# Another order of turns, scores and scale factors in the attention stage of a one-core Macaron block

## The chip, the cores and the metric

The kernel runs on one core of a Trainium2 chip. The metric is the device time of one execution in microseconds (us). Three runs of the kernel before are shown, and their median is compared.

## What is computed

One transformer block on 512 tokens of width 1024: a layer norm, half a SwiGLU feed-forward, a token mixer, and the other half feed-forward, each closed by a layer norm and modulated by nine vectors from a small product of the conditioning vector. All of it is fp32. The change is in the token mixer:

```python
z = h @ w_mix_in                   # pool, q, k/v of three branches, gates
y_a = pool_mixer(u_pool, pool_w, pool_scale) @ w_branch_a
y_b = nsa_attention(q, k_cmp, v_cmp, k_slc, v_slc, k_win, v_win, g_nsa, ...) @ w_branch_b
return (g_a * y_a + g_b * y_b) @ w_mix_out
# nsa_attention: 8 heads of 64, 2 key/value groups
#   o = g0 * softmax(q kc^T + bias) vc  +  g1 * softmax(q kslc^T + bias) vslc
#     + g2 * softmax(q kwin^T + bias) vwin
```

With 512 tokens, blocks of 64, 16 blocks selected and a window of 512, the selected and the window branch are both plain causal attention over all 512 keys. The compressed branch has 31 keys.

## The kernel before

**Weights.** Each product in fp32 is made of three: high part by high part, high by low, low by high. A panel of 128x1024 weights is loaded by the queue of SyncE into one of two `raw` buffers, ScalarE makes its high part (L1147), GpSimd its low part (L539), TensorE multiplies it with the 512 tokens (L616 to L618, 24 matmuls). Panels are taken in the order of the list `MIX`, then the branch panels (`B_BRANCH`, ...), and counted by `panels_used`. GpSimd works through its own list in order: splits, `alibi(j)` (the position bias of a pair of heads, L564), and `normalize(u)` (L574).

**Before the loop.** After panel `q3`, TensorE makes the compressed keys and values (L932, L936). VectorE copies them to `kcB` and `VC` (L1976, L1979) and counts `cmp_kv_taken`. Then follow panel `kslc`, the compressed scores of all heads (L947, waits for `cmp_kv_taken`), panel `kwin`, the scores of unit 0, panel `vslc`, the pool mixer's product, panel `vwin`, the transposes of the compressed probabilities (L998) and those of the two values (L1006, each waits until ScalarE has copied its panel out of PSUM, L1453).

**The loop.** It goes over eight units: four pairs of heads by two branches (`PAIR_UNITS`). A unit has four tiles of 128 queries, tile t with 128(t+1) keys, for two heads. For each unit and tile:

- `score(u, t)`, TensorE, L976: two products into PSUM banks 0 and 1 or 2 and 3, by turns.
- `shift(u, t)`, VectorE, L2012: adds the bias, keeps the row's extreme, writes to `Pr` in SBUF.
- `exps(u, t)`, ScalarE, L1431: the exponential, with the row's sum.
- `scales(u, part)`, VectorE, L2021 and L2023: one over the sum, times the gate, for the tiles of that part. `scales(u, 2)` also multiplies tile 3 by its factors (L2031).
- `normalize(u)`, GpSimd, L574: multiplies tiles 0, 1, 2 of both heads, six instructions.
- `turn(u, i)`, TensorE, L1027: transposes, in six turns given by `TURNS`; turn i goes to bank 4, 5 or 7 (`TURN_BANK[i % 3]`), so that turn i waits until turn i - 3 has been copied out.
- `take_turned(u, i)`, ScalarE (L1442) or VectorE (L2041): copies the turned tile to `PT`.
- `weigh(u)`, TensorE, L1054, for the first branch of a pair with L1041 ahead: the product with the values into bank 6. After a pair, `take_heads` (L1446 on ScalarE, L2045 on VectorE) empties the bank.

Step s of the loop handles unit s in its scores, unit s-1 in its turns and unit s-2 in `weigh`. The order of every engine is written out by hand. Before the change it is, in step s:

```text
TensorE  score(s,0) weigh(s-2) score(s,1) score(s,2) turn(s-1,0..3) score(s,3) turn(s-1,4) turn(s-1,5)
VectorE  shift(s,0) scales(s-1,2) shift(s,1) take(2) shift(s,2) scales(s,0) take(3) [heads] shift(s,3) scales(s,1)
ScalarE  exps(s,0) [heads] take(0) take(1) exps(s,1) exps(s,2) take(4) take(5) [split] exps(s,3)
GpSimd   normalize(s-1), then an alibi or a split in some steps
```

In step 8, which has no scores, panel `B_BRANCH` stands where the scores would. After the loop come the branch panels and `weigh(7)`.

Of the kernel before, what the change touches and what calls it, by code (L numbers as in the profile page):

```python
# [35 lines left out]
P = 128  # L36
# [25 lines left out]
       "vslc", "poolw", "vwin"]  # L62
# [25 lines left out]
TURNS = [(0, (0, 1)), (1, (0, 1)), (3, (0,)), (3, (1,)), (2, (0,)), (2, (1,))]  # L88
# [88 lines left out]
def build(nc, xT, cols, ada_w, ada1, ffn_in, ffn_out, mix_w, pool_w, branch_w, mixout_w,  # L177
          w1, w2, pos, ident_in, dist_in, cbias_in, cmask_in, icnt_in, out):
    with ExitStack() as ctx:
# [349 lines left out]
        def _(gp):  # L529
# [37 lines left out]
            def normalize(u):  # L567

                for t in range(TT - 1):
                    gp.wait_ge(scales_made, 3 * u + 1 + t // 2)  # L570
# [41 lines left out]
        def _(pe):  # L612
# [328 lines left out]
            k8_panel("kslc")  # L941
            pe.wait_ge(cmp_kv_taken, 2)
            pe.wait_ge(act_evac, MIX8.index("q3") - 1)
            for t in range(TT):
# [4 lines left out]
                if t % 2:  # L949
                    ins.then_inc(cmp_scored, 1)  # L950
            k8_panel("kwin")
# [31 lines left out]
            pe.wait_ge(shifted, 6)  # L983
# [9 lines left out]
            k8_panel("vwin")  # L993
# [8 lines left out]
            pe.wait_ge(shifted, 8)  # L1002
            for v in range(2):
                pe.wait_ge(act_evac, MIX8.index("vslc") - 1 + v)
                for t in range(TT):
                    ins = pe.transpose(psum[:, 2 + v, P * t:P * t + P], vT[:, v, t * P:(t + 1) * P], ident[:, :])  # L1006
                ins.then_inc(v_turned, 1)

            def turn(u, i):
# [22 lines left out]
            def weigh(u):  # L1032
# [10 lines left out]
                pe.wait_ge(turned_act, 4 * u + 4)  # L1043
                pe.wait_ge(turned_dve, 2 * u + 2)
# [14 lines left out]
            for s in range(1, NPU + 1):  # L1059
# [14 lines left out]
                turn(s - 1, 4)  # L1074
                turn(s - 1, 5)

            for m in range(KT):
                p = B_BRANCH + 3 * m
                b = 4 * (m % 2)
                if m >= 2:  # L1080
                    pe.wait_ge(br_mixed, m - 1)
                if m == 1:
                    pe.wait_ge(o_split, HPG)
                if m:
                    panel_over_h(p, p % 4, b)
# [48 lines left out]
        def _(act):  # L1134
# [281 lines left out]

            def take_k(br, name):
# [3 lines left out]
            take_k(0, "kslc")  # L1421
            act.wait_ge(cmp_shifted, 1)
            act.activation(Pc[:, :, :, 0:N_CMP], Pc[:, :, :, 0:N_CMP], ACT.Exp).then_inc(cmp_exp, 1)
# [794 lines left out]
```

## Time and profile before

| | |
|---|---|
| median of 3 runs | 1132.77 us (1132.46 to 1132.92) |
| the profiled execution | 1132.92 us, span 1131.1 us |
| TensorE busy | 1106.7 us, 98% of the span |
| GpSimd, VectorE, ScalarE busy | 529.4, 512.6, 409.3 us |
| attention loop, 500.47 to 569.52 us | 69.05 us, TensorE busy 62.98 us |

The span is from the first to the last instruction. Busy time is the union of an engine's instructions. A wait is idle time of an engine just ahead of an instruction, with what ended it. In a timeline each row is one instruction or a run of equal ones: start, length, engine, line, operation, output and inputs, count, and in brackets the idle time ahead and its releaser. The first shape of a run stands for all of it.

### The profile page before, as it was taken

How to read it: one execution, taken by the hardware profiler on the slowest of the kernel's cores; microseconds unless marked ns; L12 is line 12 of the kernel's file. 1: busy time of each engine (PE TensorE's matmuls, PEld its weight loads, DVE VectorE, ACT ScalarE, POOL GpSimd, SP SyncE). 2: the span in 40 equal slices, each digit the busy share in tenths (PEclk: the TensorE clock that was granted, in tenths of full speed). 3: DMA queues.
4: the chain of work that ended last, by engine and by line, in shares of the span. 5: the costliest groups of instructions: out<-in, count | busy, mean ns of one | idle time of the engine just before them, and what ended most of it. 6: DMA issues, size and time to landing. Idle time of an engine off the chain costs nothing.

```text
span 1131.1 us, 15426 instructions
## 1 busy us (share of the span) xinstructions
PE 1106.7 (98%) x5596; PEld 905.2 (80%) x5596; DVE 512.6 (45%) x888; ACT 409.3 (36%) x649; POOL 529.4 (47%) x274
## 2 busy tenths in 40 slices
PE   7999999999999999999999999999999999999997
PEld 4788888888888897865578888888888888888886
DVE  5577755311221368368837775774322221211113
ACT  4452332233222283267723232347232222322222
POOL 1435544444445464459814543546544544444440
PEclk9999999999999999999999999999999999999999
DMA  9455554323333262210036654323443333233322
GB/s 374 153 190 209 185 191 168 102 94 96 88 90 99 79 249 92 84 36 21 22 128 214 202 174 155 112 75 112 134 136 121 111 111 96 90 98 91 99 68 75
DMA packets 52372, 142.13 MB, mean 126 GB/s; under 512 B 5728, under 2 KB 11872, under 8 KB 51040
## 3 DMA queue, kind: packets, MB, share of 16 engines
q1 hardware_dynamic: 51312, 136.25, 36.6%
q10 hardware_dynamic: 1008, 5.17, 1.2%
q8 instruction: 34, 0.56, 0.2%
q14 instruction: 18, 0.15, 0.0%
HBM read 139.31 MB, written 2.10 MB: 125 GB/s over the span
## 4 chain that ended last, share of the span: by engine, by line
PE 93%; DVE 4%; issue 1%; ACT 1%; DMA 0%; ACTq 0%; DVEq 0%
PE psum L616 29%; PE psum L618 28%; PE psum L617 28%; PE psum L1054 2%; PE psum L1027 1%; PE psum L976 1%; PE psum L911 1%; PE psum L633 1%; PE psum L647 0%; DMA X<-in_xT 0%; DVE Pr L2012 0%; DVE X L1664 0%; PE psum L668 0%; DVE scr L1604 0%; PE psum L723 0%
## 5 line engine op out<-in xcount | busy, mean ns | idle before, releaser
L539 POOL TENSOR_TENSOR w_lo<-raw,w_hi 128x1024 fp32r<-128x1024 f32 x184 | 452.8, 2465 | 535.1 <-ACT w_hi L1147 534.7
L616 PE MATMUL psum<-h_hi,w_hi 128*128 128x512 f32 (+1 forms) x1016 | 384.9, 379 | 1.3 <-DVE h_lo L1677 0.8
L618 PE MATMUL psum<-h_hi,w_lo 128*128 128x512 f32 (+1 forms) x1016 | 381.9, 376 | 0.0
L617 PE MATMUL psum<-h_lo,w_hi 128*128 128x512 f32 (+1 forms) x1016 | 381.7, 376 | 0.0
L1147 ACT ACTIVATE w_hi<-raw 128x1024 fp32r<-128x1024 f32 x184 | 192.9, 1051 | 150.6 <-PE psum L618 99.0
L616 PEld LDWEIGHTS psum<-h_hi,w_hi 128*128 128x128 f32 x1016 | 191.1, 188 | 40.1 <-issue 3.0
L618 PEld LDWEIGHTS psum<-h_hi,w_lo 128*128 128x128 f32 x1016 | 191.1, 188 | 35.1
L617 PEld LDWEIGHTS psum<-h_lo,w_hi 128*128 128x128 f32 x1016 | 191.2, 188 | 33.9
L1760 DVE SCALAR_TENSOR_TENSOR acc<-ada_raw,cact,acc 128x512 f32<-128x512 f32 x98 | 137.7, 1440 | 18.1 <-DMA ada_raw<-in_ada_w 17.9
L616 PE MATMUL psum<-act_hi,w_hi 128*128 128x512 f32 (+1 forms) x374 | 141.4, 378 | 0.9 <-issue 0.9
L618 PE MATMUL psum<-act_hi,w_lo 128*128 128x512 f32 (+1 forms) x374 | 140.9, 377 | 0.0
L617 PE MATMUL psum<-act_lo,w_hi 128*128 128x512 f32 (+1 forms) x374 | 140.8, 377 | 0.0
L1830 DVE SCALAR_TENSOR_TENSOR X<-psum,mod,X 128x512 f32<-128x512 f32 x20 | 15.0, 750 | 194.9 <-PE psum L618 194.9
L1317 ACT ACTIVATE act_hi<-scr 128x512 f32 (+1 forms) x42 | 26.6, 632 | 190.6 <-DVE scr L1791 190.6
L616 PEld LDWEIGHTS psum<-act_hi,w_hi 128*128 128x128 f32 x374 | 70.4, 188 | 14.0 <-issue 1.3
L1781 DVE SCALAR_TENSOR_TENSOR scr<-scr,psum 128x512 f32<-128x512 f32 x44 | 30.1, 685 | 113.0 <-ACT scr L1324 113.0
L618 PEld LDWEIGHTS psum<-act_hi,w_lo 128*128 128x128 f32 x374 | 70.4, 188 | 13.0
L617 PEld LDWEIGHTS psum<-act_lo,w_hi 128*128 128x128 f32 x374 | 70.4, 188 | 12.7
L1791 DVE TENSOR_TENSOR scr<-scr,psum 128x512 f32<-128x512 f32 x44 | 30.2, 686 | 92.9 <-PE psum L618 92.7
L1324 ACT ACTIVATE scr<-psum 128x512 f32<-128x512 f32 x44 | 26.1, 594 | 88.3 <-PE psum L618 88.3
L1772 DVE TENSOR_TENSOR act_lo<-scr,act_hi 128x512 f32 (+1 forms) x44 | 33.2, 754 | 36.3 <-ACT act_hi L1317 34.9
L574 POOL TENSOR_SCALAR Pr<-Pr,pscl 128x128 f32<-128x128 f32 (+2 forms) x48 | 44.9, 955 | 8.9 <-DVE pscl L2023 8.8
(240 smaller groups left out, 1000.8 us busy)
## 6 DMA issues: line engine op xcount, KB each, us to landing
raw<-in_ffn_in SPq DMA_DIRECT2D x82, 512.0 KB, 3.3
ada_raw<-in_ada_w SPq DMA_DIRECT2D x112, 256.0 KB, 3.5
raw<-in_ffn_out SPq DMA_DIRECT2D x32, 448.0 KB, 3.4
raw<-in_mix_w SPq DMA_DIRECT2D x27, 512.0 KB, 3.3
ada_first<-in_ada SPq DMA_DIRECT2D x8, 1024.0 KB, 11.5
raw<-in_ffn_out SPq DMA_DIRECT2D x16, 512.0 KB, 3.5
raw<-in_branch_w SPq DMA_DIRECT2D x8, 512.0 KB, 4.0
raw<-in_mixout_w SPq DMA_DIRECT2D x8, 512.0 KB, 3.3
```

What stands on the lines that cost most here:

```text
L539: gp.tensor_tensor(w_lo[:, slot, :], raw[:, slot % 2, :], w_hi[:, slot, :].bitcast(F32), ALU.subtract).then_inc(split_done, 1)
L574: gp.tensor_scalar(pr, pr, pscl[:, n:n + 1], None, ALU.mult).then_inc(probs_pool, 1)
L616: pe.matmul(o_, w_hi[:, wslot, ws], xh, start=first, stop=False)
L617: pe.matmul(o_, w_hi[:, wslot, ws], xl, start=False, stop=False)
L618: return pe.matmul(o_, w_lo[:, wslot, ws], xh, start=False, stop=last)
L1147: act.activation(w_hi[:, slot, :], raw[:, slot % 2, :], ACT.Copy).then_inc(split_hi, 1)
L1317: act.activation(act_hi[:, c - 1, :] if isinstance(c, int) else act_hi[:, bass.ds(c - 1, 1), :].rearrange("p o t -> p (o t)"), scr[:, 1 - ...
L1324: act.activation(scr[:, c2, :], bank(2 * c2 if b is None else b), ACT.Tanh, scale=0.5).then_inc(tanh_done, 1)
L1760: dve.scalar_tensor_tensor(a, ada_raw[:, q % 3, :], sc, a, ALU.mult, ALU.add).then_inc(ada_used, 1)
L1772: dve.tensor_tensor(lo_, scr[:, b, :], hi.bitcast(F32), ALU.subtract).then_inc(act_split, 1)
L1781: dve.scalar_tensor_tensor(scr[:, c2, :], scr[:, c2, :], 1.0, bank(b0), ALU.add, ALU.mult).then_inc(gated, 1)
L1791: dve.tensor_tensor(scr[:, c2, :], scr[:, c2, :], bank(b0 + 1), ALU.mult).then_inc(hidden_made, 1)
```

## The change

- `MIX`: `vwin` is taken before `poolw`, and TensorE runs `vslc`, `vwin`, the transposes of the values, and only then the pool product and the transposes of the compressed probabilities. VectorE's copies follow that order.
- TensorE makes the compressed scores straight after the compressed keys and values; panel `kslc` follows them.
- VectorE finishes the compressed probabilities before the shifts of unit 0 instead of after them.
- `TURNS` takes tile 2 (turns 2 and 3) before tile 3 (turns 4 and 5). VectorE copies out turns 0, 1 and 5, ScalarE 2, 3 and 4.
- `scales` has two parts instead of three: tiles 0 to 2, then tile 3. The first is issued after `take_turned(s-1, 5)`, ahead of `shift(s, 3)`. `normalize` waits once, for the first part.
- Step 8 of the loop has no panel; `B_BRANCH` comes after the loop, ahead of `B_BRANCH + 1` and `weigh(7)`.

In step s of the loop the orders become:

```text
TensorE  score(s,0) weigh(s-2) score(s,1) turn(s-1,0) turn(s-1,1) score(s,2) turn(s-1,2..5) score(s,3)
VectorE  shift(s,0) scales(s-1,1) shift(s,1) take(0) take(1) shift(s,2) take(5) [heads] scales(s,0) shift(s,3)
ScalarE  exps(s,0) [heads] exps(s,1) take(2) take(3) take(4) exps(s,2) [split] exps(s,3)
```

The core of the diff:

```diff
-       "vslc", "poolw", "vwin"]
+       "vslc", "vwin", "poolw"]
...
-TURNS = [(0, (0, 1)), (1, (0, 1)), (3, (0,)), (3, (1,)), (2, (0,)), (2, (1,))]
+TURNS = [(0, (0, 1)), (1, (0, 1)), (2, (0,)), (2, (1,)), (3, (0,)), (3, (1,))]
...
+                gp.wait_ge(scales_made, 2 * u + 1)
                 for t in range(TT - 1):
-                    gp.wait_ge(scales_made, 3 * u + 1 + t // 2)
...
-            k8_panel("kslc")
             pe.wait_ge(cmp_kv_taken, 2)
...
+            k8_panel("kslc")
             k8_panel("kwin")
...
             k8_panel("vslc")
-            pe.wait_ge(shifted, 6)
+            k8_panel("vwin")
+            pe.wait_ge(shifted, 8)
+            for v in range(2):
+                pe.wait_ge(act_evac, MIX8.index("vslc") - 1 + v)
+                for t in range(TT):
+                    ins = pe.transpose(psum[:, 2 + v, P * t:P * t + P], vT[:, v, t * P:(t + 1) * P], ident[:, :])
+                ins.then_inc(v_turned, 1)
...
-                elif i in (0, 5):
-                    pe.wait_ge(turned_dve, 2 * u + i // 5)
+                elif i in (0, 1, 5):
+                    pe.wait_ge(turned_act, 3 * u + (-1, 0, 0, 0, 0, 1)[i])
                 else:
-                    pe.wait_ge(turned_act, 4 * u + (0, -1, 0, 1, 2)[i])
+                    pe.wait_ge(turned_dve, 3 * u + i - 2)
...
                 if s < NPU:
                     score(s, 1)
+                turn(s - 1, 0)
+                turn(s - 1, 1)
+                if s < NPU:
                     score(s, 2)
-                else:
-                    pe.wait_ge(shifted, 8 * NPU)
-                    panel_over_h(B_BRANCH, B_BRANCH % 4, 0)
-                for i in range(4):
+                for i in range(2, 6):
                     turn(s - 1, i)
                 if s < NPU:
                     score(s, 3)
-                turn(s - 1, 4)
-                turn(s - 1, 5)
...
-                ts = (slice(0, 2), slice(2, 3), slice(3, 4))[part]
+                ts = slice(0, 3) if part == 0 else slice(3, 4)
...
+            for v in range(2):
+                dve.wait_ge(v_turned, v + 1)
+                dve.tensor_copy(V[:, v, :, :].rearrange("p t c -> p (t c)"), bank(2 + v)).then_inc(v_taken, 1)
             for g in range(4):
                 dve.wait_ge(poolout_hi, g + 1)
...
                 if s <= NPU:
-                    take_turned(s - 1, 2)
+                    take_turned(s - 1, 0)
+                    take_turned(s - 1, 1)
                 if s < NPU:
                     shift(s, 2)
-                    scales(s, 0)
                 if s <= NPU:
-                    take_turned(s - 1, 3)
+                    take_turned(s - 1, 5)
                 if s >= 3 and s % 2:
                     take_heads((s - 3) // 2)
                 if s < NPU:
+                    scales(s, 0)
                     shift(s, 3)
-                    scales(s, 1)
```

## Rows read from the trace of the kernel before

**Rows 1.** The page of the profile: the span, and the busy time of each engine.

```profile
span 1131.1 us, 15426 instructions
...
PE 1106.7 (98%) x5596; PEld 905.2 (80%) x5596; DVE 512.6 (45%) x888; ACT 409.3 (36%) x649; POOL 529.4 (47%) x274
```

**Rows 2.** The waits of TensorE over the span: total us, times, longest us.

```profile
PE psum L1041 <- DVE o_lo L2045: 2.1, 3, 1.0
PE psum L1054 <- ACT PT L1442: 2.0, 3, 0.7
...
PE psum L1054 <- DVE PT L2041: 1.0, 1, 1.0
PE psum L976 <- DVE V L2072: 0.9, 1, 0.9
```

**Rows 3.** Busy time by stretch: the attention loop, then steps 4 and 5 of it.

```profile
500.47:569.52 69.05, 62.98 (x405) 37.08 (x405) 53.69 (x188) 47.49 (x145) 57.42 (x52) 1.00 0.11 36
524.58:533.77 9.19, 8.62 (x57) 4.69 (x56) 7.67 (x28) 6.30 (x21) 8.57 (x9) 1.00 0.00 0
533.77:542.08 8.31, 7.62 (x53) 4.50 (x52) 6.68 (x27) 7.63 (x23) 7.96 (x8) 1.00 0.00 0
```

**Rows 4.** Timeline, TensorE: compression products, the kslc panel's start, compressed scores.

```profile
467.23 0.63 PE L936 MATMUL psum<-w2s,hidden 128*31 128x64 f32 x8
467.80 0.50 PE L616 MATMUL psum<-h_hi,w_hi 128*128 128x512 f32 x1
...
473.37 3.68 PE L947 MATMUL psum<-kcB,qT 128*128 128x62 f32 x32
```

**Rows 5.** Timeline, VectorE: the four copies into VC.

```profile
468.33 1.17 DVE L1979 TENSOR_SCALAR VC<-psum 31x128 f32<-31x128 f32 x4
```

**Rows 6.** Timeline, TensorE and ScalarE: what follows the vwin panel; its copy from PSUM.

```profile
498.63 1.03 PE L998 MATMUL psum<-ident,Pc 128*128 128x128 f32 x8
...
498.83 0.60 ACT L1453 ACTIVATE vT<-psum 128x512 f32<-128x512 f32 x1 [3.81 <-PE psum L618]
```

**Rows 7.** Timeline, TensorE, in step 5 of the loop.

```profile
534.96 2.38 PE L1054 MATMUL psum<-PT,V 128*64 128x512 f32 x16 [0.69 <-ACT PT L1442]
...
538.54 1.75 PE L1027 MATMUL psum<-ident,Pr 128*128 128x128 f32 x14
540.22 1.13 PE L976 MATMUL psum<-kT,qT 64*128 64x512 f32 x4
```

**Rows 8.** Timeline, the other engines in the same steps.

```profile
532.85 0.62 ACT L1431 ACTIVATE Pr<-Pr,nmax 128x384 f32<-128x384 f32 x1
...
533.41 0.17 DVE L2023 TENSOR_TENSOR pscl<-pscl,G 128x4 f32<-128x4 f32 x1
...
533.68 5.61 POOL L574 TENSOR_SCALAR Pr<-Pr,pscl 128x128 f32<-128x128 f32 x6 [0.45 <-DVE pscl L2023]
...
533.97 0.19 ACT L1431 ACTIVATION_READ_ACCUMULATOR Pr<-Pr,nmax 128x1 f32 x1
...
539.08 1.03 ACT L1442 ACTIVATE PT<-psum 128x256 f32<-128x256 f32 x2 [0.56 <-PE psum L1027]
```

**Rows 9.** Groups by shape, 505 to 562 us: count, then busy us and mean ns.

```profile
L1431 ACT ACTIVATE Pr<-Pr,nmax 128x512 f32<-128x512 f32 x14 | 10.0, 714 | 3.5 <-DVE nmax L2012 3.5
...
L2012 DVE CUSTOM_DVE_ANT_0 Pr<-psum,abias 128x512 f32<-128x512 f32 x14 | 9.0, 681 | 0.0
...
L1431 ACT ACTIVATE Pr<-Pr,nmax 128x256 f32<-128x256 f32 x14 | 6.9, 498 | 0.0
...
L1442 ACT ACTIVATE PT<-psum 128x512 f32<-128x512 f32 x6 | 3.6, 598 | 0.3
```

**Rows 10.** Duration in ns, min/median/max: the scales' product; VectorE's normalising of tile 3.

```profile
L2023 DVE TENSOR_TENSOR pscl<-pscl,G x24: 160/163/2180, 486.7 to 563.0; 128x2 f32<-128x2 f32 x16, 128x4 f32<-128x4 f32 x8
...
L2031 DVE TENSOR_SCALAR Pr<-Pr,pscl x16: 485/794/811, 488.6 to 563.9; 128x512 f32<-128x512 f32 x16
```

More of the change, by code:

```diff
@@ L991, in _ @@
             ins.then_inc(panels_used, 1)
-            k8_panel("vwin")
             pe.wait_ge(cmp_probs, 1)
@@ L1001, in _ @@
                 ins.then_inc(cmp_PT, 1)
[L1002 to L1007, printed above, removed]
             def turn(u, i):
@@ L1081, in _ @@
                     pe.wait_ge(br_mixed, m - 1)
+                if m == 0:
+                    pe.wait_ge(shifted, 8 * NPU)
                 if m == 1:
                     pe.wait_ge(o_split, HPG)
-                if m:
-                    panel_over_h(p, p % 4, b)
+                panel_over_h(p, p % 4, b)
                 panel_over_h(p + 1, (p + 1) % 4, b + 1)
@@ L1415, in _ @@
             take_q(3)
-            def take_k(br, name):
+            act.wait_ge(cmp_shifted, 1)
+            act.activation(Pc[:, :, :, 0:N_CMP], Pc[:, :, :, 0:N_CMP], ACT.Exp).then_inc(cmp_exp, 1)
+            for br, name in enumerate(("kslc", "kwin")):
                 wait_used(taken(name))
                 act.activation(kT[:, br, :], bank(MIX_BANK[name]), ACT.Copy).then_inc(act_evac, 1)
-            take_k(0, "kslc")
-            act.wait_ge(cmp_shifted, 1)
-            act.activation(Pc[:, :, :, 0:N_CMP], Pc[:, :, :, 0:N_CMP], ACT.Exp).then_inc(cmp_exp, 1)
-            take_k(1, "kwin")
             def exps(u, t):
@@ L1449, in _ @@
                 exps(0, t)
-            def take_v(v, name):
-                act.wait_ge(panels_used, taken(name))
+            for v, name in enumerate(("vslc", "vwin")):
+                wait_used(taken(name))
                 act.activation(vT[:, v, :], bank(MIX_BANK[name]), ACT.Copy).then_inc(act_evac, 1)
-            split_before(taken("vslc"))
-            take_v(0, "vslc")
             for g in range(4):
@@ L1460, in _ @@
                                scale=colv[:, C_PSCALE + g:C_PSCALE + g + 1]).then_inc(poolout_hi, 1)
-            split_before(B_BRANCH - 1)
-            take_v(1, "vwin")
             for s in range(1, NPU + 1):
@@ L1468, in _ @@
                     take_heads((s - 3) // 2)
-                take_turned(s - 1, 0)
-                take_turned(s - 1, 1)
                 if s < NPU:
                     exps(s, 1)
+                for i in range(2, 5):
+                    take_turned(s - 1, i)
+                if s < NPU:
                     exps(s, 2)
-                take_turned(s - 1, 4)
-                take_turned(s - 1, 5)
                 if s in (4, 6):
@@ L2001, in _ @@
             dve.tensor_tensor(Pm, Pm, over_blocks(cst[:, 0, :]), ALU.subtract).then_inc(cmp_shifted, 1)
+            dve.wait_ge(gates_taken, 1)
+            seen = cmask[:, :, 0:1].broadcast_to([P, TT, HEADS])
+            link(dve.tensor_tensor(cst[:, 2, :].rearrange("p (t h) -> p t h", t=TT), G[:, :, 0:24:3], seen, ALU.mult))
+            dve.wait_ge(cmp_exp, 1)
+            link(dve.tensor_reduce(cst[:, 1, :], Pv, AX.X, ALU.add))
+            link(dve.reciprocal(cst[:, 1, :], cst[:, 1, :]))
+            link(dve.tensor_tensor(cst[:, 2, :], cst[:, 1, :], cst[:, 2, :], ALU.mult))
+            dve.tensor_tensor(Pm, Pm, over_blocks(cst[:, 2, :]), ALU.mult).then_inc(cmp_probs, 1)
             def shift(u, t):
@@ L2025, in scales @@
                                   G[:, ts, c:c + 3 * HPG + 1:3 * HPG], ALU.mult).then_inc(scales_made, 1)
-                if part == 2:
-                    dve.wait_ge(scales_made, 3 * u + 3)
+                if part == 1:
+                    dve.wait_ge(scales_made, 2 * u + 2)
                     for hd in range(2):
@@ L2069, in _ @@
                 dve.tensor_copy(PcT[:, g, :], bank(4 + g)).then_inc(cmp_PT_taken, 1)
-            for v in range(2):
-                dve.wait_ge(v_turned, v + 1)
-                dve.tensor_copy(V[:, v, :, :].rearrange("p t c -> p (t c)"), bank(2 + v)).then_inc(v_taken, 1)
             for s in range(1, NPU + 2):
@@ L2077, in _ @@
                 if 2 <= s <= NPU:
-                    scales(s - 1, 2)
+                    scales(s - 1, 1)
                 if s < NPU:
```

13 lines of the change are left out of this document (2 added, 11 removed).

## The prediction

> **What bounds the kernel now.** I read the page first: TensorE is busy for 1106.7 of 1131.1 us [rows 1], and it is the chain that ends last. So the change can give or take only what TensorE waits. Its waits by line come next: those that touch the change are 2.1 us at L1041, 2.0 and 1.0 at L1054, 0.9 at L976 [rows 2], 6.0 together. The windows put them in the attention loop: 69.05 us long, 62.98 busy, so 6.07 us idle; the granted clock there is 1.00, the level of 2.4 GHz [rows 3]. Step 4, with the compressed product, holds 8.62 us of work in 9.19, step 5 holds 7.62 in 8.31 [rows 3]: the mean step has 8.12 us of work and 0.63 of waiting. Nothing else that is edited touches a wait of TensorE today. The timelines of one step then give the prices [rows 4 to 8].
>
> **The parts ahead of the loop.** *Compressed scores before `kslc`.* L936 ends at 467.86 and `kslc` starts at 467.80 (starts overlap ends a little) [rows 4]. The scores wait for `cmp_kv_taken`, and the last of VectorE's copies to `VC` ends at 468.33 + 1.17 = 469.50 [rows 5]. Today the panel, 473.37 - 467.80 = 5.57 us, hides this. Moved ahead of it, the scores start at about 469.55: **+1.75 us**. Behind the waiting TensorE stand `kslc`, `kwin` and the scores of unit 0; all move by as much. What is late next: nothing, since ScalarE's exponential and VectorE's sums get the `kslc` and `kwin` panels as cover, 11 us. For the same reason the compressed probabilities, moved ahead of unit 0's shifts on VectorE, cost nothing; without that cover they would hold back the shifts by some 3 us.
>
> *`vwin` and the value transposes ahead of the pool product.* ScalarE starts to copy `vwin` 0.20 us after the panel's end (498.63, where the next product starts) and needs 0.60 [rows 6]. Today the compressed transposes cover it. Now only the four transposes of `vslc` stand between, 0.48 at 0.12 each (14 of them take 540.22 - 538.54 = 1.68 us [rows 7]). **+0.35 us**: 0.85 - 0.48.
>
> *The first step of the loop.* Today TensorE waits 0.9 us in it for VectorE's copies of V [rows 2]. Now those are done early, but the pool product stands right ahead, and VectorE's four subtractions and two copies behind it have to end before `shift(1, 0)`, on which `score(1, 2)` waits for its bank. I found about 0.8 to 1.0 us; I let it cost 0.9, as today. Bounds: 0 and 2.
>
> **The loop.** The gain that the change has is plain. Today `weigh` waits 0.69 us for ScalarE's last copy [rows 7] or for `take_heads`. With `score(s, 3)` behind the last turn there is about 1.1 us more of cover [rows 7], and these waits, 0.6 to 1.0 in each of steps 2 to 8, go.
>
> But a new cycle appears. `scales(s, 0)` now needs the exponentials of tile 2; on ScalarE these stand behind the copy of turn 4; turn 4 stands on TensorE behind turn 3, and turn 3 needs the last of GpSimd's six multiplications of unit s-1, which start only with `scales(s-1, 0)`. Today none of these steps closes the circle: GpSimd starts on tiles 0 and 1 before tile 2 is known, and turn 2 is a tile that VectorE normalises. One turn round this ring:
>
> - from the end of `scales` to GpSimd's start: 533.68 - 533.58 = 0.10 [rows 8]
> - six multiplications: 5.61 [rows 8]
> - from GpSimd to TensorE: not seen as a wait in the trace. Between 0 and 0.2, the size of the other handovers here; I take 0.1
> - turn 3 (three transposes) and turn 4 (four): 0.84
> - to ScalarE's copy: the first turn's two transposes begin at 538.54, end at 538.78, and the copy starts at 539.08 [rows 7, 8]: 0.30
> - copy of 512 columns: 0.60 [rows 9]
> - two exponentials of 384: 532.85 to 534.16: 1.31 [rows 8]
> - reciprocal and product of `scales`, twice 0.17 and the gap between [rows 8]: 0.40
>
> Sum 9.26; I use **9.25 us** a step, 9.0 to 9.5 with the bounds. TensorE has 8.12, so GpSimd's chain is the new bound. Other edits of the loop lie within it: VectorE has the copies of turns 0, 1, 5 instead of 2 and 3, the same engine's work of about 7 us a step [rows 3]; `scales(s-1, 1)` and the normalising of tile 3 end some 4 us after the ring's start, and their turn comes at 6.2. An alibi or a split of GpSimd, up to 3 us, fits in the 3.6 us for which it waits in the ring.
>
> From the end of `score(1, 3)` to that of `score(7, 3)` there are six rounds, 55.5 us. TensorE's work in them is 3 x 8.62 + 3 x 7.62 = 48.7 [rows 3]: 6.8 us of waiting. Step 8: `score(7, 3)` ends 1.05 us before `scales(7, 0)` does; then 0.1 + 5.61 + 0.1 to turn 3, and turns 3, 4, 5 take 1.32: 8.2 us, with `weigh(6)` 2.3, the compressed product 1.0 [rows 3] and 2.4 of transposes as work: 2.4 us of waiting. Panel `B_BRANCH`, which stood in this step, is only moved. It sat ahead of the turns and hid this wait; without it nothing does. After the loop `weigh(7)` comes after the same sum of work as today, so what hangs on it (VectorE's units of the modulation, SyncE's loads) keeps its place.
>
> **The sum.** Waits in the loop: 0.9 + 6.8 + 2.4 = 10.1, less 6.07 now: +4.0. With 1.75 and 0.35: +6.1. I take off 0.1 for roundings: **+6.0 us**. The profiled execution has 1132.92 us, 1.8 more than its span, and gives 1138.9; the median is 0.15 below it: **1138.8 us**.
>
> **A rule weighed.** VectorE's product in `scales` has a median of 0.163 us, and once took 2.18 [rows 10], while GpSimd subtracted 1024 columns. With GpSimd's multiplications under way it is mostly the short value; the normalising of tile 3 beside them varies from 0.485 to 0.811. The Trainium skill (SBUF — State Buffer, "Who interferes with whom") has a VectorE instruction with two SBUF inputs, or in a two-port mode, shut out for the whole of a GpSimd instruction that reads SBUF. The trace agrees for the one long case and not for most of the others.
>
> **Rivals.**
> - *The ring does not close as I say, and the next one binds.* It runs between VectorE and ScalarE: `shift(s-1, 3)` to its first half, 0.7, two exponentials of 512, 1.5 [rows 9], `scales` 0.4, normalising 1.4 [rows 10], half of `shift(s, 1)` 0.45, two exponentials of 256 1.0, three copies 1.45, two exponentials of 384 1.31, `scales` 0.4: 8.6 us. For it speaks that GpSimd's times are rough; against it, that 5.6 us for six tiles returns in every step. 6.0 - 6 x 0.6 = +2.4: 1135.2 us.
> - *Faster.* The last turn's copy leaves the path, and no ring is longer than TensorE's 8.12 us. Left are 2.1 us ahead of the loop, 0.9 in step 1 and 1.0 at the end, less 6.07: -2.0 us, 1130.8. It decides for faster once a round takes less than 8.25 us, 1.0 below my sum; GpSimd alone has 5.6 of it, and the copy and the exponentials 1.9. I see no term that could lose so much.
> - *GpSimd shuts VectorE out.* `scales(s-1, 1)` and the normalising fall under GpSimd's multiplications. If they waited for whole instructions, by the 2 us of the one long case, VectorE's copy of turn 1 would come 1.5 us after turn 4's place, and each round grow by that: +9 more, 1148 us. Against it: both already lie under GpSimd's work today, at a median of 0.163 and 0.794 [rows 10].
>
> **How the numbers follow.** Chances: forecast 0.71, the next ring 0.16, faster or even 0.08, shut out 0.05. The forecast's own range, by the ring's bounds (six rounds by 0.25) and the first step's, is 1136.9 to 1140.6. Eight times in ten: from 1134.8, with the next ring in it, to 1141.0. About 0.2%, 2.3 us, is what a measurement of this kernel can tell from no change. Slower by more: the forecast, the shut-out and a third of the next ring, 0.81. Within: the rest of that ring and part of the even case, 0.14. Faster: 0.05.
>
> **What would show it.** Right: L947 starts about 1.7 us after L936 ends; in steps 2 to 7 the times between two `score(s, 3)` are near 9.25 for odd and even steps alike; TensorE waits at L1027 for GpSimd's L574, and no longer at L1054 for L1442; GpSimd starts 0.1 us after `scales` in each step. The loop with its waits has 10 us idle. Wrong: steps of 8.3 and 8.6 us (a ring of another kind), waits at L976 for VectorE's shift, or a wait at L947 that is not there because the copies to `VC` are quicker.

## The result

The changed kernel takes 1141.61 us (median of 4 runs, 1141.44 to 1141.84) where the kernel before takes 1132.85 beside it (1132.46 to 1134.3): a ratio of 1.0076, with an interval of 1.0057 to 1.0093. It is slower, as forecast, by 8.8 us where 6.0 were forecast. 1138.8 was named, with a range to 1141.0, and the time lies 0.6 above it. The question of the experiments is where the 2.8 us more come from; the answer begins with the fact that the forecast's 6.0 was not right in its parts either.

The profiled execution took 1139.34 us, 2.3 less than the median; what the record says of that difference stands under "Open" below. The page of the profile of after, to be held against [rows 1]:

```profile
span 1137.3 us, 15410 instructions
PE 1111.6 (98%) x5596; PEld 907.3 (80%) x5596; DVE 515.3 (45%) x880; ACT 407.0 (36%) x641; POOL 530.0 (47%) x274
```

TensorE has the same 5,596 matmuls and is **busy for 4.9 us more**: 1111.6 against 1106.7. A change that only moves work can't do that if a matmul always takes the same time. Its idle time rose by only 1.3 us (1137.3 - 1111.6 = 25.7, before 24.4). The waits of TensorE from 440 to 600 us, to be held against [rows 2] (total us, times, longest us):

```profile
PE psum L1027 <- POOL Pr L574: 2.6, 5, 0.7
PE psum L1027 <- DVE PT L2037: 1.9, 3, 0.6
PE psum L946 <- DVE VC L1966: 1.7, 1, 1.7
PE psum L1041 <- DVE o_lo L2041: 0.7, 3, 0.4
PE psum L1027 <- DVE PcT L2057: 0.7, 2, 0.5
PE psum L988 <- ACT vT L1446: 0.3, 1, 0.3
```

The waits at L1054 are gone. New are those of the turns (L1027), the 1.7 at the compressed scores (L946, the line that was L947) and the 0.3 at the value transposes (L988): 7.9 us in all, 1.9 more than before. The 1.9 us that are put down to VectorE's copies (`PT` L2037) are turn 3's in the odd steps, and by the times it is GpSimd that they wait for too: at 545.17 turn 3 needs the copy of turn 0, the first of two copies that last from 544.12 to 545.13, and the last of GpSimd's six multiplications, which ends at 545.12.

Waits alone don't explain the result. TensorE's timeline at the compressed scores does, against [rows 4]:

```profile
466.67 0.63 PE L936 MATMUL psum<-w2s,hidden 128*31 128x64 f32 x8
468.98 5.96 PE L946 MATMUL psum<-kcB,qT 128*128 128x62 f32 x32 [1.68 <-DVE VC L1966]
474.70 0.77 PE L616 MATMUL psum<-h_hi,w_hi 128*128 128x512 f32 x1
475.27 0.63 PE L617 MATMUL psum<-h_lo,w_hi 128*128 128x512 f32 x1
...
476.98 0.45 PE L618 MATMUL psum<-h_hi,w_lo 128*128 128x512 f32 x1
477.26 0.39 PE L616 MATMUL psum<-h_hi,w_hi 128*128 128x512 f32 x1
```

The same 32 products took 3.68 us before, and take 5.96 here. The first matmuls of `kslc` behind them take 0.77 and 0.63 us; from 477.26 on they take 0.39 again. The windows of the same stretch show TensorE's granted clock, the share of full speed that the chip lets it have (bounds in us, length, then busy us and instructions of PE, PEld, DVE, ACT and POOL, then that clock, DMA share, GB/s):

```profile
468.00:470.00 2.00, 1.02 (x9) 1.02 (x10) 1.14 (x5) 0.00 (x0) 0.00 (x0) 1.00 0.00 0
470.00:472.00 2.00, 2.00 (x13) 2.00 (x12) 0.36 (x2) 0.00 (x0) 0.00 (x0) 0.56 0.00 0
...
474.00:476.00 2.00, 2.00 (x8) 1.81 (x8) 0.99 (x3) 0.00 (x0) 0.00 (x0) 0.50 0.00 0
476.00:480.00 4.00, 4.00 (x16) 3.19 (x16) 2.90 (x4) 1.80 (x2) 0.00 (x0) 0.86 0.02 4
480.00:490.00 10.00, 10.00 (x50) 7.38 (x49) 6.27 (x17) 4.43 (x13) 5.40 (x2) 1.00 0.31 105
```

TensorE stands still for 1.68 us, starts again, and 1.3 us later its granted clock falls from 1.00 (2.4 GHz) to 0.50 (1.2 GHz). The shares of the windows say how long: 0.56 in the second window means that 0.24 of its 2 us ran at 1.00, so the fall is at 470.24; 0.86 in the fourth means 1.1 of 4 us at 0.50, so the return is at about 477.1. **6.8 to 6.9 us at half clock.** It works without a gap at half speed, so half of that, **3.4 us**, is lost. The same work ran at 1.00 before. (The Trainium skill, TensorE: Matmul & The Clock Gate, "What's actually happening", has these two levels and a clock that drops when the engine has been idle and returns when it has been busy; the trace agrees in kind, with the fall coming behind 1.68 us of idleness.)

The loop is better than forecast. One round of it, first TensorE with its three starts of `score(s, 3)` and the last turns between:

```profile
528.46 1.35 PE L976 MATMUL psum<-kT,qT 64*128 64x512 f32 x8
...
535.57 1.99 PE L1027 MATMUL psum<-ident,Pr 128*128 128x128 f32 x14
537.49 1.35 PE L976 MATMUL psum<-kT,qT 64*128 64x512 f32 x8
...
546.52 1.35 PE L976 MATMUL psum<-kT,qT 64*128 64x512 f32 x8
```

and the other engines in the same round, to be held against [rows 8]:

```profile
530.23 0.17 DVE L2019 TENSOR_TENSOR pscl<-pscl,G 128x6 f32<-128x6 f32 x1
...
530.50 5.58 POOL L574 TENSOR_SCALAR Pr<-Pr,pscl 128x128 f32<-128x128 f32 x6 [3.44 <-DVE pscl L2019]
...
532.87 0.17 DVE L2019 TENSOR_TENSOR pscl<-pscl,G 128x2 f32<-128x2 f32 x1
533.08 1.40 DVE L2027 TENSOR_SCALAR Pr<-Pr,pscl 128x512 f32<-128x512 f32 x2
...
536.21 1.60 ACT L1436 ACTIVATE PT<-psum 128x384 f32<-128x384 f32 x3 [0.27 <-PE psum L1027]
537.71 0.61 ACT L1425 ACTIVATE Pr<-Pr,nmax 128x384 f32<-128x384 f32 x1
...
538.31 0.60 ACT L1425 ACTIVATE Pr<-Pr,nmax 128x384 f32<-128x384 f32 x1
...
539.03 0.19 DVE L2017 RECIPROCAL pscl<-psumv 128x6 f32<-128x6 f32 x1 [0.68 <-ACT Pr L1425]
539.26 0.17 DVE L2019 TENSOR_TENSOR pscl<-pscl,G 128x6 f32<-128x6 f32 x1
...
539.53 0.60 POOL L574 TENSOR_SCALAR Pr<-Pr,pscl 128x128 f32<-128x128 f32 x1 [0.30 <-DVE pscl L2019]
```

This is the ring of the prediction, link by link: `scales` ends at 530.40, GpSimd works from 530.50 to 536.08, the copies on ScalarE last to 537.8, its exponentials to 538.9, `scales` again, GpSimd again at 539.53. That is 9.03 us after 530.50. The seven starts of `score(s, 3)` run from 510.60 to 564.58, six rounds of 9.00 on average, odd and even alike. Beside GpSimd's multiplications VectorE's product takes its 0.17 and the two normalisings 1.40. Nothing is held for a whole instruction of GpSimd here, so there is no shut-out; but the normalisings are not free of GpSimd either, since in a kernel of the experiments, with GpSimd idle, they take 0.49 and 0.48 us (at 554.5), and here 0.68 and 0.80. Step 8 has two waits:

```profile
571.04 0.55 PE L1027 MATMUL psum<-ident,Pr 128*128 128x128 f32 x3 [0.72 <-POOL Pr L574]
572.26 1.42 PE L1027 MATMUL psum<-ident,Pr 128*128 128x128 f32 x11 [0.67 <-POOL Pr L574]
```

**Where the time went, by position.** From the start of L936 to the first score of the loop: 500.47 - 467.23 = 33.24 us before, 505.37 - 466.67 = 38.70 after, +5.5. From there to `weigh(7)`, with the same work in both: 577.65 - 500.47 = 77.18 before, 584.51 - 505.37 = 79.14 after, +2.0. Together +7.4. The two spans differ by 6.2, because the changed kernel's profiled execution was 0.6 ahead when it reached L936, where nothing is edited yet, and took 0.7 less behind `weigh(7)`. The first +5.5 are 1.9 of waiting (1.68 and 0.25) and 3.5 of busy time for the same work (36.77 against 33.24), which is the clock. The forecast had +2.1 and +4.0.

The windows of this second stretch, and of steps 4 and 5 in it, say something that the forecast didn't expect (same columns as above; before, the first of them had 71.08 busy of 77.18, the others stand in [rows 3]):

```profile
505.37:584.51 79.14, 73.07 (x449) 42.91 (x448) 54.87 (x185) 48.59 (x143) 56.40 (x51) 1.00 0.10 31
...
528.46:537.49 9.03, 8.84 (x58) 4.67 (x57) 7.67 (x26) 6.10 (x20) 6.91 (x7) 1.00 0.00 0
537.49:546.52 9.03, 7.98 (x53) 4.46 (x53) 7.08 (x25) 7.40 (x22) 8.65 (x9) 1.00 0.01 2
```

TensorE is idle for 6.1 us in it, as before (77.18 - 71.08 = 6.1). What grew is its *busy* time, by 2.0, at a clock of 1.00. The timeline tells why. In step 8 of the kernel before, 20 transposes stand in one row and take 2.71 us. In step 5 of the changed kernel the same 20 come in four groups, with waits and a score between: 0.44 + 0.66 + 0.55 + 1.42 = 3.07, and the 0.36 between them is also what step 5 has more (7.98 against 7.62). In a row each matmul starts before the one ahead has ended (above, those of `kslc` are 0.39 us long and start 0.23 apart); a wait ends that. So a stall that is cut into small ones shows up in part as work, and a group of records with more time for the same count is a wait in disguise (1.99 for 14 transposes at 535.57, 1.75 in [rows 7]).

### The profile page after: what moved, and what is told of

It is laid out like the page before. It is cut to its first block, busy times and chain, and to the rows that moved or that the text cites. A ratio compares the mean times of both kernels' runs of the same rounds, so it can differ in the third digit from the quotient of the medians.

```text
span 1137.3 us, 15410 instructions
## 1 busy us (share of the span) xinstructions
PE 1111.6 (98%) x5596; PEld 907.3 (80%) x5596; DVE 515.3 (45%) x880; ACT 407.0 (36%) x641; POOL 530.0 (47%) x274
## 4 chain that ended last, share of the span: by engine, by line
PE 90%; DVE 4%; ACT 2%; issue 1%; POOL 1%; DMA 0%; ACTq 0%; DVEq 0%; POOLq 0%
PE psum L616 28%; PE psum L617 28%; PE psum L618 28%; POOL Pr L574 1%; ACT Pr L1425 1%; PE psum L1027 1%; PE psum L911 1%; PE psum L1054 1%; PE psum L633 1%; PE psum L976 1%; PE psum L946 1%; PE psum L647 0%; ACT PT L1436 0%; DVE X L1651 0%; DMA X<-in_xT 0%
## 5 line engine op out<-in xcount | busy, mean ns | idle before, releaser
L539 POOL TENSOR_TENSOR w_lo<-raw,w_hi 128x1024 fp32r<-128x1024 f32 x184 | 453.5, 2468 | 536.0 <-ACT w_hi L1146 535.6
```

Source lines behind the costliest of these rows:

```text
L539: gp.tensor_tensor(w_lo[:, slot, :], raw[:, slot % 2, :], w_hi[:, slot, :].bitcast(F32), ALU.subtract).then_inc(split_done, 1)
```

## The experiments

Two theories at the start. **Clock**: what the forecast missed is TensorE's half-speed stretch, set off by the wait that the change puts in front of the compressed scores. **Ring or rest**: it is a wait of the loop, or of the parts behind it, that the profiled execution shows too short. Each kernel was timed in five rounds beside the kernel before, whose median was 1133.3 to 1133.5. The first four of the table were timed together, and so were the next four and the last four; kernels of different series are best compared by their ratios.

| kernel | median us (range) | ratio (interval) |
|---|---|---|
| after, again | 1140.83 (1140.20 to 1141.57) | 1.0066 (1.0052 to 1.0080) |
| after, `kslc` back ahead | 1138.47 (1137.17 to 1140.44) | 1.0047 (1.0034 to 1.0061) |
| before, scores ahead of `kslc` | 1138.46 (1138.05 to 1139.79) | 1.0045 (1.0031 to 1.0059) |
| after, wait filled with matmuls | 1137.69 (1137.00 to 1138.38) | 1.0038 (1.0024 to 1.0051) |
| before, new loop alone | 1135.64 (1135.35 to 1136.09) | 1.0016 (1.0007 to 1.0025) |
| after, scales in three parts | 1149.79 (1146.04 to 1150.32) | 1.0133 (1.0117 to 1.0149) |
| after, GpSimd longer | 1147.21 (1143.46 to 1148.41) | 1.0122 (1.0107 to 1.0137) |
| after, panel in step 8 | 1139.83 (1138.61 to 1141.03) | 1.0053 (1.0041 to 1.0065) |
| after, half of `kslc` ahead | 1137.54 (1136.98 to 1138.48) | 1.0036 (1.0024 to 1.0048) |
| after, three parts, split behind the normalising | 1139.52 (1135.45 to 1141.25) | 1.0046 (1.0029 to 1.0063) |
| all three remedies | 1135.54 (1134.72 to 1137.34) | 1.0022 (1.0013 to 1.0031) |
| before's parts ahead, new loop mended | 1134.54 (1133.61 to 1135.17) | 1.0005 (0.9996 to 1.0013) |

**The changed kernel once more**, unedited.

> The changed kernel once more, to see a second trace. Its profiled execution had 1139.3 us, its timed ones 1141.4 to 1141.8. Theory A (the clock makes the difference): TensorE's granted clock falls to 0.5 after the wait of 1.7 us ahead of the compressed scores, and stays there for a time that differs between executions; this trace shows a longer or a second stretch at 0.5 where its time is nearer 1141.5. Theory B (something late in the kernel): the stretch at 0.5 is 6.9 us again whatever the time, and the further 2 us lie behind the attention loop.

1140.83 us, +7.5. The stretch at half clock was there again, 6.8 us long by the records, in a profiled execution of 1140.20 us. This decides neither way between the theories: the 0.9 us more than in the first profile came with no longer stretch, and they did not lie behind the loop either, since this execution reached L936 at 467.67, 1.0 later than the first, ahead of everything that was edited.

**`kslc` back ahead of the compressed scores**, in the changed kernel (ScalarE's order goes back with it):

```diff
+            k8_panel("kslc")
             pe.wait_ge(cmp_kv_taken, 2)
...
-            k8_panel("kslc")
             k8_panel("kwin")
```

> The changed kernel with panel kslc back ahead of the compressed scores. Theory A: the wait of 1.7 us and the stretch at half clock (3.3 us lost in the trace) both go; left are 0.25 us for the turn of vwin and 2.0 us in the loop: 1135 to 1136 us, granted clock 1.000 throughout. Rival (the loop costs most, as the prediction had it, +4): 1137 to 1138 us.

1138.47 us, 2.4 less than the changed kernel beside it. The wait at the scores is gone, they take 3.68 us, the clock stays at 1.00. But more had been expected, and TensorE's waits show what stands against it:

```profile
PE psum L976 <- DVE nmax L2012: 2.4, 1, 2.4
```

Unit 0's scores wait for VectorE's shifts. The changed kernel puts the compressed probabilities ahead of these shifts, and the prediction had said that this costs nothing only under the cover of both panels, and some 3 us without it. With `kslc` back in front of the scores half of the cover is gone, and 2.4 us appear. So the two edits belong together, and undoing one alone brings out the price of the other.

**The scores ahead of `kslc`, alone**, in the kernel before: the reverse edit, nothing of the loop.

```diff
-            k8_panel("kslc")
             pe.wait_ge(cmp_kv_taken, 2)
...
+            k8_panel("kslc")
             k8_panel("kwin")
```

> The kernel before with the compressed scores alone moved ahead of panel kslc. Theory A: +5 to +7 us over the kernel before (1.7 of wait, 3.3 or more of half clock), 1138 to 1140 us. If the wait alone counted: +1.7 us, 1134.5.

1138.46 us, +5.2 to the kernel before (+5.1 by the ratio of 1.0045). The forecast's price for this one edit was 1.75. Timeline and windows of this kernel show the wait of the prediction, and then the clock:

```profile
469.50 4.95 PE L946 MATMUL psum<-kcB,qT 128*128 128x62 f32 x32 [1.68 <-DVE VC L1975]
```

```profile
472.00:474.00 2.00, 2.00 (x11) 2.00 (x11) 0.35 (x2) 0.00 (x0) 0.00 (x0) 0.50 0.00 0
```

1.68 of waiting and 3.4 of half clock are 5.1. One edit of one panel's place carries more than half of the whole loss.

**The wait filled.** The changed kernel, with eight matmuls that compute nothing anyone reads, in the time in which TensorE waited. They fill the 1.88 us from the end of L936 to the scores where 1.68 were idle; if only waiting counted, this kernel would be 0.2 us slower.

```diff
+            for i in range(8):
+                pe.matmul(bank(6), w_hi[:, pf % 4, i * P:(i + 1) * P], h_hi[:, i, :], start=(i == 0), stop=(i == 7))
             pe.wait_ge(cmp_kv_taken, 2)
```

> The changed kernel with eight more matmuls of 128x512 (useless work into a bank that is free) in the place of the wait, 1.8 us by 0.227 each. Theory A (the idle wait makes the clock fall): granted clock 1.000, so 3.3 us or more faster than the changed kernel, about 1136.5 to 1138. Rival (the small products around, of 31 and 62 columns, make it fall, not the wait): the stretch at 0.5 stays and the time is that of the changed kernel, 1141.5.

1137.69 us: **3.1 less than the changed kernel beside it, with more work in it.** The products are as fast as ever, with no wait ahead of them:

```profile
470.02 3.68 PE L951 MATMUL psum<-kcB,qT 128*128 128x62 f32 x32
```

The granted clock is 1.00 from there to the end of the loop. This is the plainest evidence for the clock theory: what the idleness cost beyond itself is some 3.1 + 0.2 = 3.3 us. It also speaks against the rival that the small products around, of 31 to 64 columns, bring the clock down wherever they stand: they are all still there.

The timed executions agree. For each the record has the mean granted clock: 0.995 to 0.997 in all of the changed kernel and of the one with the scores alone moved, and 0.998 to 1.000 in all of those without a wait at the scores (`kslc` back, filled, and half of `kslc` ahead, below).

**What the length of a wait does not tell.** A wait of this length is not enough. In the kernel before, and in every other kernel here, TensorE waits 1.7 us once more, far behind the attention, and in the kernel with `kslc` back it waits 2.4 us for the shifts:

```profile
737.69 0.39 PE L616 MATMUL psum<-mixed_hi,w_hi 128*128 128x256 f32 x1 [1.67 <-DVE scr L1622]
```

```profile
486.34 1.13 PE L976 MATMUL psum<-kT,qT 64*128 64x512 f32 x4 [2.37 <-DVE nmax L2012]
```

Behind neither did the clock fall in any of the profiled executions. These two stand between products of 256 to 512 columns, the one at the scores between products of 31 to 64 columns. Whether that is the difference was not tested. Nor is there a kernel with these small products in one row and no wait: wherever the clock stayed up, larger products stood in the wait's place. What is shown is that they keep it up there.

**The new loop alone**: the kernel before up to the loop, the changed kernel from there.

> The kernel before with the loop's part of the change alone: TURNS, copies, two parts of scales, no panel in step 8. Everything ahead of the loop is as before. By the trace of the changed kernel the loop costs +2.0 us: 1134.9 us, steps of 9.0. By the prediction's ring of 9.25: +4.0, 1136.8 us.

1135.64 us, +2.1 to the median beside it, +1.8 by the ratio. That is the loop's price, 4.0 in the forecast, and the profile's position count gave 2.0. Its waits for the ring are like those of the changed kernel, 2.7 and 2.5:

```profile
PE psum L1027 <- POOL Pr L574: 2.7, 5, 0.7
PE psum L1027 <- DVE PT L2037: 2.5, 4, 0.6
```

**`scales` in three parts**, as before the change, in the changed kernel: GpSimd starts on tiles 0 and 1 without tile 2, and the ring is opened there.

```diff
-                gp.wait_ge(scales_made, 2 * u + 1)
                 for t in range(TT - 1):
+                    gp.wait_ge(scales_made, 3 * u + 1 + t // 2)
...
-                ts = slice(0, 3) if part == 0 else slice(3, 4)
+                ts = (slice(0, 2), slice(2, 3), slice(3, 4))[part]
```

> The changed kernel with scales in three parts again, tiles 0 and 1 right behind shift(s, 2), tile 2 ahead of shift(s, 3), so that GpSimd starts early. If the ring over GpSimd's six multiplications binds (theory of the prediction): steps of 8.5 to 8.6, the next ring, 0.4 to 0.5 less in each of six, 2.5 to 3 us faster than the changed kernel. If the ring between VectorE and ScalarE binds already (rival): steps stay at 9.0 and the time with them.

1149.79 us, 7.6 to 9.0 more than the changed kernel (by the ratios and by the medians), against the expectation of every theory. The first rounds are short, 8.65 and 8.55 us, so the ring does open; the next takes 9.40. Then come TensorE's long waits, the first of which is

```profile
547.05 2.58 PE L1027 MATMUL psum<-ident,Pr 128*128 128x128 f32 x11 [3.14 <-DVE PT L2037]
```

and on VectorE and GpSimd, just before:

```profile
542.51 3.37 DVE L2027 TENSOR_SCALAR Pr<-Pr,pscl 128x512 f32<-128x512 f32 x2
...
543.09 2.52 POOL L539 TENSOR_TENSOR w_lo<-raw,w_hi 128x1024 fp32r<-128x1024 f32 x1
```

Since GpSimd is early, its subtraction for a split panel (L539) falls beside VectorE's normalising of tile 3, and two normalisings take 3.37 us instead of 1.40. This is the third rival, the shut-out, which did not happen in the loop of the changed kernel. And with TensorE's wait of 3.14 the clock falls as with the other one, as the windows show:

```profile
547.00:555.00 8.00, 7.95 (x27) 4.08 (x29) 5.89 (x23) 5.29 (x17) 5.43 (x6) 0.50 0.15 58
570.00:580.00 10.00, 9.09 (x27) 3.92 (x29) 6.70 (x24) 5.26 (x15) 5.43 (x6) 0.52 0.01 2
```

The whole first window is at half clock. Windows around it (0.81 from 544 to 548, 0.91 from 556 to 560) put the stretch at 546.5 to 556.7, 10.2 us, and there is a second one of 10.2, from 570.4 to 580.6, with a wait of 2.79. (The Trainium skill, SBUF — State Buffer, "Who interferes with whom", says that VectorE and GpSimd share a pair of SBUF ports which one of them holds for a whole instruction; here a subtraction of 1024 columns does shut VectorE out, while multiplications on GpSimd beside the same normalising, above, only lengthen it from 0.48 to 0.68 or 0.80 us.)

**One more operation on GpSimd** for each unit, a multiplication of 128 columns by one ahead of the six, 0.60 us, in the changed kernel:

```diff
                 gp.wait_ge(scales_made, 2 * u + 1)
+                pr = Pr[:, u % 2, 0, 0:P]
+                gp.tensor_scalar(pr, pr, ones[:, 0:1], None, ALU.mult).then_inc(probs_more, 1)
+                gp.wait_ge(probs_more, u + 1)
```

> The changed kernel with one more GpSimd instruction of 128 columns (a multiplication of tile 0 by one) ahead of each unit's six, about 0.6 to 0.7 us. If GpSimd is in the ring that binds: each of six steps and the end grow by it, +4 to +5 us. If the other ring binds with GpSimd near it: less than +2.

1147.21 us, 6.4 more than the changed kernel by the two medians, where 4 to 5 were expected. The starts of `score(s, 3)` run from 507.32 to 566.01: 9.78 a round against 9.00. From the start of the added operation to the first of the six, which now take 5.67, pass 0.70 us; with the 0.09 by which the six are longer that is 0.79, and the round grew by 0.78. So the slope is one: GpSimd's chain is what binds, all of it. Six rounds make 4.7 us of the 6.4. The waits say the same:

```profile
PE psum L1031 <- POOL Pr L578: 9.0, 13, 1.4
```

In this profiled execution the 32 products behind the same wait of 1.68 took 3.78 us and the clock did not fall there. It took 1143.46 us with a mean granted clock of 0.998; its three others took 1147.17 to 1148.41 with 0.992 to 0.994, so the clock fell in them, and for longer than in the changed kernel (0.995 to 0.997). That is room enough for the time over the 4 to 5 us.

**The panel back in step 8**, in the changed kernel:

```diff
+                else:
+                    pe.wait_ge(shifted, 8 * NPU)
+                    panel_over_h(B_BRANCH, B_BRANCH % 4, 0)
                 turn(s - 1, 0)
```

> The changed kernel with panel B_BRANCH back in step 8, ahead of unit 7's turns. The trace of the changed kernel has waits of 0.72 and 0.67 us at those turns; both go: -1.4 us. If step 8's waits cost nothing elsewhere hidden: 0.

1139.83 us, 1.0 less than the changed kernel of the first series (1.5 by the two ratios), where 1.4 was expected. The waits of step 8 for GpSimd are gone. Here the half clock lasted longer in the profile:

```profile
468.94 6.11 PE L946 MATMUL psum<-kcB,qT 128*128 128x62 f32 x32 [1.68 <-DVE VC L1968]
```

and behind it matmuls of 512 columns still took 0.63 us at 479.65: 10.2 us at half clock, or 5.1 lost.

**Half of `kslc` ahead of the scores**, half behind, in the changed kernel, to cover the wait with half a panel.

```diff
+            for k in range(4):
+                product(bank(MIX_BANK["kslc"]), pk % 4, k, h_hi[:, k, :], h_lo[:, k, :], k == 0, False)
             pe.wait_ge(cmp_kv_taken, 2)
...
-            k8_panel("kslc")
+            for k in range(4, KT):
+                ins = product(bank(MIX_BANK["kslc"]), pk % 4, k, h_hi[:, k, :], h_lo[:, k, :], False, k == KT - 1)
+            ins.then_inc(panels_used, 1)
```

> The changed kernel with panel kslc cut in two around the compressed scores: its first 12 matmuls (2.7 us) run while VectorE copies to kcB and VC, its last 12 behind the scores. No work is added or left out. Theory A (an idle TensorE loses 1.7 us, and 0, 3.4 or 5.1 us more to the clock, by the execution): no wait at L946, granted clock 1.000 around it, 4 to 6 us faster than the changed kernel: 1135 to 1136.5 us. Rival (the clock falls for the small products themselves, and the eight idle matmuls of the filled kernel only masked it): a stretch at 0.5 is left, 1138 or more.

1137.54 us: 3.3 less than the changed kernel, no wait at the scores, no half clock, but 1 us above the 1135 to 1136.5 that were expected. TensorE waits 1.8 us for VectorE's shifts, and the cause is on VectorE and GpSimd:

```profile
480.62 1.78 DVE L2003 TENSOR_TENSOR cst<-cst 128x32 f32<-128x32 f32 x1
482.43 3.29 DVE L2004 TENSOR_TENSOR Pc<-Pc,cst 128x992 f32<-128x992 f32 x1
```

```profile
479.94 4.73 POOL L539 TENSOR_TENSOR w_lo<-raw,w_hi 128x1024 fp32r<-128x1024 f32 x2 [13.28 <-ACT w_hi L1153]
```

The probabilities' products stand for as long as GpSimd's two subtractions last: 1.78 us for 32 columns, and 3.29 for 992, which in the changed kernel take 1.19. The cover was too short for that.

**Three parts, with the split behind the normalising**: the kernel of three parts, and GpSimd's split in units 4 and 6 waits until VectorE has normalised.

```diff
                         if u in (4, 6):
+                            gp.wait_ge(probs_dve, 2 * u + 2)
                             split(B_BRANCH + u // 2, (B_BRANCH + u // 2) % 4)
```

> The changed kernel with scales in three parts, and GpSimd's two weight splits of steps 5 and 7 held back until VectorE has normalised tile 3. Theory L (in the run without the guard GpSimd's TENSOR_TENSOR of 1024 columns shut VectorE's normalising out for 2.5 us, and the 3.1 and 2.8 us of waiting at L1027 and two stretches at half clock came of it): both waits and both stretches go, 1138 to 1140 us, steps of 8.6 to 8.8. Rival (three parts are slow for another reason): 1146 or more.

1139.52 us: **some 10 less than without this one wait.** The long waits and their half clock are gone; the longest for VectorE's copies is 1.0 now. So the shut-out was the cause of the loss, and a semaphore wait on GpSimd its cure. What remains is the half clock at the compressed scores, 10.2 us long in this profile. One of its six executions took only 1135.45 us, with a mean granted clock of 0.999; the five others took 1138.47 to 1141.25, with 0.995 or 0.996: the same kernel with and without the fall. The rounds are not the 8.6 to 8.8 that were expected: 8.65, 8.54, 9.41, 8.70, 9.06 and 9.05, 8.90 on average against 9.00 in the changed kernel.

**All three remedies**: half of `kslc` ahead, three parts with the wait, the panel in step 8.

> The changed kernel with three edits: kslc cut in two around the scores, scales in three parts with the guard, panel B_BRANCH in step 8. By the sum of the parts: -5 (no wait, no half clock), -1 to -2 (steps of 8.6 to 8.8 instead of 9.0), -1.4 (step 8): 1132 to 1134 us, level with the kernel before.

1135.54 us, above the 1132 to 1134 that were expected. By the ratios it is 5.0 better than the changed kernel and still 2.5 behind the one before. 1.8 of these are the wait of unit 0's scores for the shifts, again in its trace.

**The mended loop on the old parts ahead of it**: the kernel before up to the loop, then the changed loop with three parts, the wait and the panel.

> The kernel before up to the loop, and the changed loop with three parts of scales, the guard and panel B_BRANCH in step 8. If the next ring of 8.6 us binds in all six steps, the mean step is 0.15 shorter than the 8.75 of the kernel before, and the wait of step 8 (1.0) is less: 1131.5 to 1133, about 1 us faster than before. If some steps stay near 9: 1133 to 1134.

1134.54 us, ratio 1.0005: no difference that the interval lets one tell. A gain of 1 us had been expected. The waits at L1054 that the change set out from are gone, and in their place stand

```profile
PE psum L1028 <- DVE PT L2040: 2.7, 5, 1.1
...
PE psum L977 <- DVE V L2070: 0.9, 1, 0.9
PE psum L1042 <- DVE o_lo L2044: 0.7, 3, 0.4
PE psum L1028 <- POOL Pr L574: 0.6, 1, 0.6
```

4.9 us, where the kernel before has 6.0 in its loop. Its six rounds take 9.49, 8.75, 9.41, 8.70, 9.06 and 9.06 us, 9.08 on average, no less than in the changed kernel: here the three parts did not shorten the rounds at all. What it has over the new loop alone (1.0005 against 1.0016) is of the size of what the panel in step 8 gave. Even mended, the new order has nothing to give that five rounds of timing could see.

## Why the prediction was right in direction and wrong in size

- **Compressed scores, +1.75.** The wait is there with 1.68 us, at the place and for the copies that were named. *This is the step that failed*: "Moved ahead of it, the scores start at about 469.55: +1.75 us" priced the edit as waiting alone, at the clock of 1.00 of the rows before. TensorE's clock fell to 0.50 behind it and cost 3.4 us more in both profiled executions of the changed kernel. In those of the edited kernels that have the same wait it cost 3.4 in two, 5.1 in two, and nothing in one. The edit alone costs 5.1, and filling the wait with useless work takes 3.1 off the whole. No rival had the clock in it.
- **What is late next: nothing.** Right for the change as a whole: L976 waits for no shift. The condition that was put to it held as well: with the cover of `kslc` away the shifts hold TensorE for 2.4 us ("some 3"). With half of it away it was 1.8, and there GpSimd's subtractions had a part in it.
- **Value transposes, +0.35.** 0.25.
- **First step, 0.9.** 0.53 + 0.19 = 0.7.
- **The ring.** Right in kind: the steps are even, TensorE waits at L1027 for GpSimd and no longer at L1054, GpSimd starts 0.10 us behind `scales`, and its time goes into the round one to one. The size was 9.25 and is 9.03. From GpSimd's end at 536.08 to the first exponential at 537.71 pass 1.63 us, where two handovers, the turns and a copy had been given 0.1 + 0.84 + 0.30 + 0.60 = 1.84; the other terms came within 0.03. Six rounds of 9.00 instead of 9.25 make 1.5 us.
- **Step 8, 2.4** (the terms that are given for it make 2.5). The waits are 0.39 + 0.72 + 0.67 = 1.8, and from the end of `score(7, 3)` to the next panel pass 7.7 us (565.71 to 573.43), where 8.2 were forecast. Putting the panel back takes 1.0 to 1.5 off the time.
- **Waits of the loop, +4.0.** +2.0 by position, +1.8 to 2.1 timed alone. The rounds' 1.5 and the 0.5 of step 8 make up the 2.0 that are missing; in the first step the 0.2 of shorter waits go into transposes that are broken into groups (2.89 for its 20, 2.71 in a row). And the sign "the loop has 10 us idle" was wrong: it has 6.1, as before.
- **The sum.** Predicted 1.75 + 0.35 + 4.0 = 6.1. Found 1.68 + 0.25 + 2.0 = 3.9 without the clock and 7.3 to 9.0 with it, where 7.4 stands in the profile and 7.5 to 8.8 in the two timings. Two errors of opposite sign, of 2 and of 3.4 to 5.1, nearly hid each other: that the forecast missed its range by only 0.6 us is luck.
- **The rivals.** The next ring doesn't bind, nor did the kernel get faster. The shut-out did not occur in the loop of the changed kernel, at its multiplications, but it is real: at GpSimd's subtractions, once something moves them onto VectorE's work.

**Open.** Why the half clock lasts 0, 6.8 or 10.2 us behind the same wait of 1.68 was not found, nor why longer waits at other places leave the clock alone. In the two profiles with 10.2 us the fall came 1.1 us after TensorE started again, in the four with 6.8 after 1.3 to 2.4; that is all that the traces add. The 2.3 us between the changed kernel's profiled execution and the median of the others are not explained by a longer stretch alone: it would cost 1.7, and two of those four have the profiled one's mean clock, 0.996, and take 2.1 and 2.5 us more (the two others have 0.995). Some of it can lie ahead of the edits, where the profiled executions already differ by 1.3 us (L936 starts between 466.36 and 467.67), and this one was among the early ones. The rounds of 9.4 us that come back in kernels with three parts were not taken apart.

## What to carry to other kernels

A wait put in front of TensorE costs more than its length when the clock falls behind it. Its length does not tell whether that happens: here it did behind 1.68 us between small products, and did not behind 2.37 between larger ones. So look at the granted clock of the stretch; and where the clock does fall, work in the wait, even useless work, can be cheaper than idleness. When a step is moved for a stall that it has, first list the waits that it was hiding for others, since a panel in the right place covers several at once. And when an order of work looks free, ask which ring closes through the engine that now waits for its last input: the ring's sum, here within 0.25 us of the measured round, tells whether the gain can exist.

## What was not expected of the hardware

- Behind one and the same wait of TensorE, 1.68 us, its clock is at 1.2 GHz for 6.8 us (in four profiles, with 4.95 to 5.96 us for the 32 products), for 10.2 us (in two, 6.11 and 6.12) or not at all (in one, 3.78). With waits of 3.14 and 2.79 it fell as well, for 10.2 us each. Behind a wait of 1.67 to 1.68 between products of 256 columns (737.69 in the kernel before), which all fourteen profiled executions have, it never fell, nor behind 2.37, 1.81 and 1.79 at unit 0's scores in three kernels.
- The kernel before is not free of such losses: in its timed executions of the three series the mean clock goes from 1.000 down to 0.996, and the time from 1132.0 up to 1136.6 with it (1132.8 on average at 0.999 and 1.000, 1135.5 at 0.996 and 0.997).
- The one such stretch in the profile of the kernel with a longer GpSimd came at three waits of 0.75, 0.57 and 0.67 us close together; from 574 to 578 us the mean granted clock was 0.57. So no single long wait is needed.
- A subtraction of 1024 columns on GpSimd, both inputs in SBUF, holds VectorE's operations on SBUF for as long as it lasts: 1.77 us for a product of 32 columns in the changed kernel (480.94, beside a subtraction from 480.26 to 482.67), 3.29 for 992 columns, 3.37 for two normalisings of 512. Where VectorE's product of 992 columns came first (482.75 in the changed kernel), the product took its 1.19 and the next subtraction 3.00 instead of 2.41. GpSimd's multiplications by a column of scalars held nothing for a whole instruction: VectorE's small products stayed at 0.16 to 0.18 in most rounds, and a normalising took 0.61 to 0.80 instead of 0.48.
- Twenty transposes take 2.71 us in a row and 3.07 in four groups, at the same clock.
